# Six of the first MLP's last eight output tiles by seven products instead of eight, on one Trainium2 core

## The reference

```python
y_x = square(relu(modulate(x, g_pre_mlp, sh2, sc2) @ w_mlp_in)) @ w_mlp_out   # 1024 -> 4096 -> 1024
x = x + gt2 * rmsnorm(y_x, g_post_mlp)
...
proj = rmsnorm(x, norm_mix) @ w_in_2                                          # second block
k = rmsnorm((mem_h @ w_mem_kv)[:, keys], k_norm)                              # per head of 128
lb = cumsum(softmax(hg_lb_logits))                                            # lower bounds of the gates
```

## Time and profile before

| what | value |
|---|---|
| median of 3 runs | 1291.28 us (1291.2 to 1292.35) |
| the profiled execution | 1292.66 us, span 1291.4 us |
| busy share PE / PEld / DVE / ACT / POOL | 99% / 88% / 75% / 61% / 64% |
| granted TensorE clock | 1.00 throughout |
| last inner pair ends, first plain tile starts | 560.19 us |
| first half tile starts | 593.89 us |
| first half's statistic on PE | 601.45 us |
| rows of the next projection start | 606.25 us |

### The profile page before, as it was taken

One profiled execution on the slowest core, in us unless ns is written; L12 is line 12 of the kernel. 1 busy time (PEld: TensorE's weight loads), 2 busy tenths in 40 slices (PEclk: granted clock), 3 DMA queues, 4 the chain that ended last, 5 costly groups with the idle time before them and its releaser, 6 DMA issues.

```text
span 1291.4 us, 22880 instructions
## 1 busy us (share of the span) xinstructions
PE 1279.4 (99%) x8718; PEld 1136.7 (88%) x8718; DVE 965.1 (75%) x1685; ACT 781.8 (61%) x1488; POOL 824.5 (64%) x592
## 2 busy tenths in 40 slices
PE   9999999999999999999999999999999999999998
PEld 6788778879999999988788788777789999999998
DVE  5796795878778989834468575747589887987888
ACT  4532585479677585765655556645577655765664
POOL 2644334969778687656467373644378876877785
PEclk9999999999999999999999999999999999999999
DMA  9685235353333333432432122211223333333333
GB/s 378 238 311 215 88 124 210 114 180 108 122 105 101 101 99 112 173 105 98 131 100 82 47 66 66 66 66 33 66 82 114 100 99 102 108 103 115 99 105 108
DMA packets 42125, 156.35 MB, mean 121 GB/s; under 512 B 4384, under 2 KB 5152, under 8 KB 40992
## 3 DMA queue, kind: packets, MB, share of 16 engines
q1 hardware_dynamic: 41136, 151.60, 34.3%
q0 software_dynamic: 448, 2.62, 0.5%
q10 hardware_dynamic: 432, 0.67, 0.1%
HBM read 149.90 MB, written 4.19 MB: 119 GB/s over the span
## 4 chain that ended last, share of the span: by engine, by line
PE 78%; DVE 10%; POOL 5%; ACT 4%; issue 2%; DMA 1%; DVEq 0%; SPq 0%; ACTq 0%; POOLq 0%
PE bank L879 21%; PE bank L881 21%; PE bank L880 21%; PE bank L1437 2%; POOL wL L3803 2%; PE bank L928 1%; PE bank L930 1%; PE bank L929 1%; PE bank L982 1%; POOL acc L3813 1%; DVE small L2942 1%; POOL wL L3808 1%; PE bank L975 1%; PE bank L942 1%; PE bank L967 1%
## 5 line engine op out<-in xcount | busy, mean ns | idle before, releaser
L3803 POOL TENSOR_TENSOR wL<-raw,wH 128x1024 fp32r<-128x1024 f32 (+1 forms) x91 | 228.0, 2511 | 225.2 <-ACT wH L1815 222.1
L879 PE MATMUL bank<-hH,wH 128*128 128x512 f32 (+1 forms) x544 | 211.0, 388 | 1.7 <-POOL wL L3803 0.6
L881 PE MATMUL bank<-hH,wL 128*128 128x512 f32 (+1 forms) x544 | 200.6, 369 | 0.0
L880 PE MATMUL bank<-hL,wH 128*128 128x512 f32 (+1 forms) x544 | 200.4, 368 | 0.0
L3808 POOL TENSOR_TENSOR wL<-raw,wH 128x512 fp32r<-128x512 f32 (+1 forms) x120 | 154.6, 1289 | 31.1 <-ACT wH L1824 30.5
L879 PE MATMUL bank<-gH,wH 128*128 128x256 f32 x512 | 145.4, 284 | 0.3 <-POOL gL L3808 0.3
L880 PE MATMUL bank<-gL,wH 128*128 128x256 f32 x512 | 144.9, 283 | 0.0
L881 PE MATMUL bank<-gH,wL 128*128 128x256 f32 x512 | 144.9, 283 | 0.0
L1815 ACT ACTIVATE wH<-raw 128x1024 fp32r<-128x1024 f32 (+1 forms) x91 | 95.2, 1048 | 54.6 <-PE bank L881 28.3
L879 PEld LDWEIGHTS bank<-hH,wH 128*128 128x128 f32 x544 | 102.9, 189 | 25.1 <-issue 6.5
L881 PEld LDWEIGHTS bank<-hH,wL 128*128 128x128 f32 x544 | 102.6, 189 | 18.0
(11 more groups left out here) (537 smaller groups left out, 4086.1 us busy)
## 6 DMA issues: line engine op xcount, KB each, us to landing
raw<-in_wall SPq DMA_DIRECT2D x211, 512.0 KB, 3.3
rows<-in_wall SPq DMA_DIRECT2D x24, 1024.0 KB, 11.2
bra<-in_rpbw SPq DMA_DIRECT2D x8, 360.0 KB, 4.8
xq<-in_xt SPq DMA_DIRECT2D x2, 1024.0 KB, 6.8
xT<-in_xn SPq DMA_DIRECT2D x1, 2048.0 KB, 7.9
out_x<-xT SPq DMA_DIRECT2D x1, 2048.0 KB, 8.6
xT<-out_x SPq DMA_DIRECT2D x1, 2048.0 KB, 9.3
out_x<-xT SPq DMA_DIRECT2D x6, 256.0 KB, 2.4
```

The source lines that it names most:

```text
L879: matmul(o, a_h, b_h, start=first, stop=False)
L880: matmul(o, a_h, b_l, start=False, stop=False)
L881: return matmul(o, a_l, b_h, start=False, stop=last)
L3803: tt(wL[i % NHL][:, 0:n], raw[load(c) % NRAW][:, 0:n], wH[i % NHL][:, 0:n].bitcast(F32), ALU.subtract).then_inc(s.w_lo, 1)
```

## The change

The last quarter gets three outer pairs (12, 13, 14) for output tiles 0 to 5; tiles 6 and 7 stay plain and in halves. Forms 12 to 15 are now made as the others. What tiles 6 and 7 need beyond the forms, the late tokens of the even squares, is kept in `xlast` and split once (`late_high` on ACT, a rest on POOL). The keys are squared and split in two large operations (128x1024) instead of four small ones each; their statistics are two of 512 columns, after the sixth and the seventh product of pair 14, with roots of 512 columns on ACT and two scalings of 512 columns on DVE. Squares of the results go through two buffers `ysq` and are added up in `ysum` by POOL. The lower bounds are made during pairs 12 and 13. `xT` is read back in two halves after the last pair, ahead of the third chunk of the next projection.

```diff
-        if quarter < 3:
-            for j in range(4):
-                for i, odd in ((0, 0), (1, 0), (1, 1), (0, 1)):
-                    tile("w_mlp_out", 2 * j + i, range(8 * quarter + odd, 8 * quarter + 8, 2))
-        else:
-            group([("w_mlp_out", m) for m in range(2)], OUT_ORDER)
-            for m in range(2, 8):
-                tile("w_mlp_out", m, OUT_ORDER)
+        for j in range(4 if quarter < 3 else 3):
+            for i, odd in ((0, 0), (1, 0), (1, 1), (0, 1)):
+                tile("w_mlp_out", 2 * j + i, range(8 * quarter + odd, 8 * quarter + 8, 2))
+    for m in (6, 7):
+        tile("w_mlp_out", m, OUT_ORDER)
...
 # TensorE
+        KEY_PLACE = {(G - 1, 5): 0, (G - 1, 6): 1}
...
+                if (n, q) in KEY_PLACE:
+                    memory_statistic(KEY_PLACE[n, q])
...
-        outs = [claim(BANK["w_mlp_out", m]) for m in range(2)]
-        for i, k in enumerate(OUT_ORDER):
-            ...
-        for m in range(6):
-            b = BANK["w_mlp_out", m]
-            if m >= 2:
-                tile("w_mlp_out", m, OUT_ORDER, [(claim(b), XB)])
-            freed[b] = s.y_full, m + 1
-            if 0 < m < 5:
-                statistic_of_halves(f"mk{m - 1}", 256)
...
 # ScalarE, in the loop over the pairs
+            if not more:                               # the last pair, 14
+                first_product(n)
+                ahead("w_mlp_out", OUT_ORDER[0], 6, 2)
+                result_square(2)
+                result_square(3)
+                memory_root(0)
+                continue
...
             piece_high(n + 1, 2)
-            if c is not None and c < 12:
+            if c is not None:
                 sums_of_form_high(c, 0)
+            if outer_of(n) == 13:
+                late_high()
...
             piece_high(n + 1, 6)
+            if outer_of(n) == 13:
+                act.wait_ge(s.lb_v, 3)
+                activation(lb[:, 1, :], lb[:, 1, :], ACT.Exp).then_inc(s.lb_a, 1)
+                activation(lb[:, 2, :], lb[:, 2, :], ACT.Exp).then_inc(s.lb_a, 1)
+                result_square(0)
+                result_square(1)
+                memory_squares()
...
+        result_square(4)
+        result_square(5)
+        ahead("w_mlp_out", OUT_ORDER[0], 6)
+        memory_root(1)
+        act.wait_ge(s.piece_g, 5 * G)
+        for m in (6, 7):
+            act.wait_ge(s.y_full, m - 5)
+            square(tm[m - 4][:, 0:256], y[:, m, 0:256], s.sq)
...
+        def result_square(i):
+            act.wait_ge(s.y, Y.half + 24 + i + 1)
+            if i > 2:
+                act.wait_ge(s.add_g, ADD_G.f + i - 2)
+            square((ysq[i % 2] if i else ysum)[:, :], y[:, Y_ORDER[i], :], s.sq)
...
 # VectorE
+            if outer_of(n) == 12:
+                bounds_ahead()
+            if outer_of(n) == 13:
+                bounds()
...
+        added(G - 1, 2)
...
         last_tiles(0)
+        memory_key(0)
+        memory_key(1)
         dve.wait_ge(s.coef_c, 1)
-        dve.wait_ge(s.x_moved, 48)
         second_norm(0)
...
+                    dve.wait_ge(*((s.x_moved, 48) if n < 4 else (s.x_rest_in, 16)))
                     tt(b, xT[:, n, t], b, ALU.add).then_inc(s.add2, 1)
...
 # GpSimd
             if n + 1 == G:
-                ahead("w_mlp_out", 24, 0, 2)
+                pool.wait_ge(s.sums_hi, halved("mk1") + 1)
+                tt(ksqL[:, :], ksq[:, :], ksqH[:, :].bitcast(F32), ALU.subtract).then_inc(s.sums_lo, 2)
+                result_sum(1)
+                ahead("w_mlp_out", OUT_ORDER[0], 6, 2)
+                result_sum(2)
+                result_sum(3)
                 continue
...
             piece_rest(n + 1, 3)
+            if outer_of(n) == 13:
+                pool.wait_ge(s.full, FULL.b + 33)
+                rest(xlL[:, :, :], xlast[:, :, :], xlH[:, :, :], s.rest_g)
...
+        result_sum(4)
+        result_sum(5)
...
         late_squares(0)
+        ahead("w_mlp_out", OUT_ORDER[0], 6)
         ahead("w_in_2_first", 2, 14, 1)
         late_squares(1)
...
 # SyncE
-            if i == last_inner:
-                sp.wait_ge(s.prod, outer_done(2))
+            if i == first_f + 2:
+                sp.wait_ge(s.prod, 7 * G)
                 sp.wait_ge(s.x_moved, 32)
-                nc.sync.dma_start(xT[:, :, :], out).then_inc(s.x_moved, 16)
+                nc.sync.dma_start(xT[:, 0:4, :], out[:, 0:4, :]).then_inc(s.x_moved, 16)
+                nc.sync.dma_start(xT[:, 4:8, :], out[:, 4:8, :]).then_inc(s.x_rest_in, 16)
             weights_load(i)
```

More of the change, by code:

```diff
@@ L50 @@
 GROUPS = ((0, 8), (8, 16), (16, 22))
-OUT_ORDER = [24 + i for i in (0, 1, 2, 3, 4, 5, 7, 6)]
+OUT_ORDER = range(24, 32)
+Y_ORDER = (1, 0, 3, 2, 5, 4)
 def plan_weights():
@@ L146 @@
              for pair in [("inner", p) for p in range(max(0, 4 * quarter - 2), 4 * quarter + 2)]
-             + [("outer", 4 * quarter + j) for j in range(4 if quarter < 3 else 0)]]
+             + [("outer", 4 * quarter + j) for j in range(4 if quarter < 3 else 3)]]
 INNER = {i: at for at, (kind, i) in enumerate(FIRST_MLP) if kind == "inner"}
@@ L441 @@
 MULT = before(hc=8, h2=8, b=3)
-FULL = before(first=16, hm=8, h2=4, b=24, fs=22)
+FULL = before(first=16, hm=8, h2=4, b=33, fs=22)
 REST = before(first=8, hm=4, h2=8, fs=22)
-REST_G = before(first=8, hm=4, s2=4, b=24, form=4, fb=22)
+REST_G = before(first=8, hm=4, s2=4, b=33, form=4, fb=22)
 X2_S = before(x2=8, up=22)
@@ L469, in rooted @@
     return 2 * ROOTS.index(name) + 2
-HALVED = "mk0 mk1 mk2 mk3 lq".split()
+HALVED = "mk0 mk1 lq".split()
 def halved(name):
@@ L678, in build @@
     xl = at("xl", R + 92 * K, [128, 256])
+    xlast = at("xl", 88 * K, [128, 4, 256])
+    xlH = at("xlH", R + 56 * K, [128, 4, 256], F32R)
+    xlL = at("xlL", R + 60 * K, [128, 4, 256], F32R)
+    ysum = at("ysum", R + 72 * K, [128, 512])
+    ysq = [at("ysq", R + (74 + 2 * i) * K, [128, 512]) for i in range(2)]
     sS = [at("sS", R + (24 + 4 * i) * K, [128, 1024]) for i in range(2)]
@@ L1327, in tensor_program, with XB @@
             first_freed(n)
-        def XB(k):
-            return bH[:, k % 8, :], bL[:, k % 8, :], s.lo, LO.b + (k if k % 2 else k + 2)
-        outs = [claim(BANK["w_mlp_out", m]) for m in range(2)]
-        for i, k in enumerate(OUT_ORDER):
[L1334 to L1340, removed]
-        for m in range(6):
-            b = BANK["w_mlp_out", m]
-            if m >= 2:
-                tile("w_mlp_out", m, OUT_ORDER, [(claim(b), XB)])
-            freed[b] = s.y_full, m + 1
-            if 0 < m < 5:
-                statistic_of_halves(f"mk{m - 1}", 256)
+        def XB(k, i):
+            c = 12 + (k - 24) // 2
+            if k % 2:
+                return yH[:, c % 4, 256 + 256 * i:512 + 256 * i], yB[c % 4][:, i, :], s.lo, LO.b + 2 * c + 1
+            if i:
+                return xlH[:, c % 4, :], xlL[:, c % 4, :], s.rest_g, REST_G.b + 33
+            return yH[:, c % 4, 0:256], yA[c % 4][:, :], s.lo, LO.b + 2 * c + 2
         freed[2] = freed[3] = s.piece_v, 2 * G
@@ L2201, in first_result, with late_high, memory_squares, memory_root @@
             copy(y[:, m, :], sum_bank(n, (1, 3)[count - 1]), s.y)
[L2203 to L2206, removed]
+        def late_high():
+            act.wait_ge(s.relu_sq, 2 * 15)
+            act.wait_ge(s.prod, 7 * (INNER[13] + 1))
+            copy(xlH[:, :, :], xlast[:, :, :], s.full)
+        def memory_squares():
+            act.wait_ge(s.k_mem, 4)
+            activation(ksq[:, :], kvM[:, 0:2, :].rearrange("p a t -> p (a t)"), ACT.Square).then_inc(s.head_sq, 4)
+            act.wait_ge(s.head_sq, 4)
+            activation(ksqH[:, :], ksq[:, :], ACT.Copy).then_inc(s.sums_hi, 2)
+        def memory_root(i):
+            root_of(f"mk{i}", 128, kroot[:, 512 * i:512 * i + 512], bank[BANK["mk", i]])
+        def result_square(i):
[3 more added lines that the diff above has]
+            square((ysq[i % 2] if i else ysum)[:, :], y[:, Y_ORDER[i], :], s.sq)
         act.wait_ge(s.product, done("w_mlp_in", 7, 1))
@@ L2274, in scalar_program @@
                 nc.scalar.preload_act_table_set("natural_log_exp_and_others")
[L2276 to L2295, removed]
-                if m < 6:
-                    square(tm[t][:, :], y[:, m, :], s.sq)
-                    held[t] = s.add_g, ADD_G.f + m
-                else:
-                    square(tm[t][:, 0:256], y[:, m, 0:256], s.sq)
-            if 0 < m < 5:
-                if m > 1:
-                    act.wait_ge(s.mk_n, m - 1)
-                act.wait_ge(s.sums, 5 * G)
-                root(f"mk{m - 1}", 128, rs[(m - 1) % 2], 256)
-            if 0 < m < 4:
-                memory_square(m)
+        result_square(4)
[6 more added lines that the diff above has]
+            square(tm[m - 4][:, 0:256], y[:, m, 0:256], s.sq)
         root("post_a", 1024, bank[1], 256)
@@ L3246, in vector_program @@
             if c is not None:
-                if c < 12:
-                    form_sums(c)
+                form_sums(c)
                 odd_low(c)
```

(9 more changed lines are left out.)

154 lines of the change are left out of this document (69 added, 85 removed).

## The result

The changed kernel takes 1294.54 us (median of 12 runs, 1294.03 to 1295.53) against 1291.97 us for the kernel before (13 runs, 1291.2 to 1292.74). A thirteenth execution of the changed kernel, at 3634 us, is left out. The ratio is 1.0021 [1.0013, 1.0029]: slower by 0.2%, or 2.6 us. I predicted 1291.1 us and a range up to 1293.2. The time is outside it, on the side to which I had given 0.09.

The account below looks back on a forecast made before the run. PE, 99% busy, bounds the kernel. From the last inner pair's end to the first half's statistic (the marks), 20.16 + 0.39 + 20.55 = 41.10 us against 41.26, rounded to -0.2: 1291.1 us, range 1288.8 to 1293.2; z is pair 13's end.

Parts of the forecast that it names:

- the side to which I had given 0.09: Chance of a result slower by more than 0.2% (2.6 us), from x late and the unforeseen: 0.09.
- The step that failed: Pairs 12 to 14: bounds' operations and keys' roots and scalings run beside 10 us pairs, adding nothing to the path.
- The lock: Rival at the key scalings: two-SBUF-input DVE operations and POOL block each other, POOL late up to 0.8 us; chance 0.13.
- PE's list: PE in the last quarter: 33.70 us removed, 31.15 added, 2.55 less; 38.71 us between the marks if nothing waits.
- The 109 ns: Rival on the price per 256-column matmul, against 120 ns in the trace: would leave 3.57 us gained; chance 0.01.
- x came in time: Rival after the last pair: the read of `xT` lands late, norm 6.1 us late, 1297 us; chance 0.05.
- POOL's late queue: Last pair to the half's statistic: POOL's and ACT's queues make PE wait; it goes on 20.55 us after pair 13.
- Tile 6: Second wait, after pair 14: PE waits 0.56 us for POOL's low weights of tile 6; bounds 0 and 1.5.
- ACT's order: Ahead of the half's statistic: ACT's half squares stand behind a chunk's high part and a root, first ending at z + 19.7.
- POOL's sums alone: Lower bound at the half's statistic: with the half square already there, POOL's sums end at z + 19.85, no wait.
- The first wait: Start of the quarter's second outer pair, 13: POOL late, PE loses 0.39 us; bounds 0 and twice that.
- The third wait: Statistic of the first half: PE waits 1.45 us for POOL and ACT; bounds 0 and 2.9.

Follow-up runs that it names:

- experiment 3: Changed kernel with only pair 12's three bounds operations taken out (done far ahead, before the first block's norm), pair 13's kept: 1292.33 us.
- the second experiment: Changed kernel with two more 128x4 differences with two SBUF inputs added on DVE in pair 12, results unused: 1296.01 us.
- the seventh experiment: On top of experiment 1, ACT writes result squares to PSUM and DVE adds them; POOL keeps only tile 6's half square: 1289.98 us.
- experiment 1: Changed kernel with all the bounds' operations and their exponentials behind the second norm, the coefficient behind pair 14: 1292.13 us.
- experiment 6: On top of experiment 1, the high part of the next chunk on ACT goes behind the half squares of tiles 6 and 7: 1292.14 us.
- e4: Changed kernel with pair 13's bounds operations moved behind the second norm, pair 12's kept: 1294.35 us.
- e8: On top of experiment 1, three scratch differences of 128x4 with two SBUF inputs added on DVE in pair 12: 1294.40 us.

## Why the prediction was wrong

**The step that failed** is "The bounds' small operations and the keys' roots and scalings run beside 10 us pairs", priced at nothing because the last pair leaves DVE free. The reason is true of pair 14 and so of the operations of pair 13 (experiment 3). It is not true of those of pair 12, which stand ahead of DVE's weight sums for the last pair. The earlier trace rows had DVE busy 9.69 of 10.08 us in such a pair: 0.39 us of room, which three operations of 0.16 us overrun by 0.1 and two of 1.2 to 1.3 us by far. What the runs showed in place of "nothing" is 2.5 us of marks (44.04 with pair 12's operations, 41.54 and 41.52 without them).

**The lock was a rival at the wrong place.** I read its price from the earlier trace rows and gave it 0.13, but looked for it at the keys' scalings alone and took the excess for something that goes with the operation's size. It goes with the size of what POOL is running. At the scalings it was there as well, and cheap: beside them POOL's last sum took 1.69 us where the others take 1.29 to 1.30, and the half's sum 0.99 where the earlier trace rows have 0.74, together 0.64 us. In the changed kernel POOL's last sum and DVE's scalings are:

```profile
600.07 1.69 POOL L3925 TENSOR_TENSOR ysum<-ysum,ysq 128x512 f32<-128x512 f32 x1
```

```profile
599.88 0.75 DVE L3223 SCALAR_TENSOR_TENSOR kvM<-kvM,vecs,kroot 128x512 f32<-128x512 f32 x1
601.50 0.81 DVE L3223 SCALAR_TENSOR_TENSOR kvM<-kvM,vecs,kroot 128x512 f32<-128x512 f32 x1 [0.88 <-ACT kroot L1842]
```

So the two sides of the lock are both seen: whoever comes second waits, DVE in pair 12 and POOL at the scalings. In the second experiment POOL comes first at the scalings too, and there DVE waits. The Trainium skill (SBUF — State Buffer, Who interferes with whom) says this: the one that issues first has the shared ports for its whole instruction, and the other is fully blocked. The traces agree, down to operations of four elements in a partition. I had the rule and the row, and didn't go through the added DVE operations asking of each how many SBUF inputs it has and what POOL runs then. The same section of the Trainium skill says that `tensor_scalar` may also block through a mode of its own. The one with a single input in pair 13 took 1.22 us, up to the end of POOL's instruction, where the same one in the kernel before took 0.17 with POOL idle (565.09). That agrees; the reciprocal, at 0.18, wasn't held.

**What held.** PE's list: without waits the marks would be 38.71 apart, and the seventh experiment, with 0.69 us of waits, has 39.38. The distances between matmuls of 256 columns stay at 0.12 us. The 109 ns that the Trainium skill (TensorE: Matmul & The Clock Gate, Back-to-back issue gap) gives by its formula for the isolated gap are again not what the trace shows. x came in time: the read of `xT` is issued 12.3 us after z (592.13, for 10.7) and DVE's first read of it waits for no DMA. POOL's late queue: with the bounds out of the way (experiment 1) the statistic comes at z + 20.62 where I had z + 20.55. That POOL's and ACT's queues make PE wait there held; that the number came so close is luck. Tile 6 waits 0.22 us for 0.56, POOL's four sums take 6.02 us for 5.2 (0.39 of it the lock), and ACT's order, which I had as the last to end, isn't the limit (experiment 6). I had 0.70 us less if POOL's sums alone were the limit (z + 19.85), and the lock at the scalings added 0.64.

**What was mis-sized.** The first wait, taken over from the third quarter as 0.39, is 0.73 after and 0.68 to 0.76 in the experiments. Some 0.1 to 0.2 us of it lie 1.2 us ahead of pair 13's start, in the changed kernel at 568.40. POOL's two `ySL` parts of pair 12 end at 568.35, 9.40 us into the pair. Their like in the third quarter of the kernel before ended at 488.23, 9.07 us into its pair, which began at 479.16:

```profile
485.68 2.55 POOL L3808 TENSOR_TENSOR ySL<-yS,yH 128x512 fp32r<-128x512 f32 x2 [1.80 <-ACT yH L1824]
```

So 0.33 us of POOL's lateness answers to the 0.34 us of wait. That the one makes the other isn't shown, and what makes POOL later there wasn't tried. With the first experiment's 0.76 for this term my sum is 41.10 + 0.37 = 41.47, and that experiment has 41.54.

The account in us of marks: the edit of PE's list -2.55; first wait +0.7; POOL's queue ahead of the statistic some +2.1, which together leave the +0.3 of experiment 1; the lock in pair 12 +2.5; sum +2.8. The third wait was mis-sized too, 1.45 for 1.85, and in the changed kernel the weights of tile 6 made PE wait 1.19 us for 0.56, because the lateness from pair 12 came on top.

## What to carry to other kernels

Where GpSimd works without a break, price each DVE operation with two SBUF inputs (and, by one row here, a `TENSOR_SCALAR` from SBUF to SBUF) at up to one whole GpSimd instruction, however few elements it has; put such operations where GpSimd is idle, or where nothing waits for DVE. Before taking matmuls out of a list that is 99% busy, add up what the other engines must do before the next point at which PE needs them: here 2.55 us of matmuls gave nothing until the sums had left GpSimd's queue. A wait in the middle of a chain is repaired on the engine that comes last, and moving work ahead on the other one shows which that is.

## What the runs showed of the hardware

A DVE operation of 128x4 with two SBUF inputs took 0.15 to 0.16 us with POOL idle, and 1.00 to 1.55 us, up to the end of POOL's instruction, with POOL at work; one of 128x8 took 2.42 us under an instruction of 128x1024 and 0.16 with POOL idle. Where three or four stood one behind the other and POOL's instructions were back to back, the first began 0.1 to 0.2 us before POOL's instruction ended and took 0.15 to 0.19 us (after, e2, e4, e8); each of those behind it waited for one whole instruction of POOL, as long as POOL had one to run.

In the second experiment the granted clock fell. Its windows before and behind 592 us (busy PE, PEld, DVE, ACT, POOL, clock, DMA share, GB/s):

```profile
585.00:592.00 7.00, 4.60 (x34) 4.16 (x34) 6.86 (x8) 5.22 (x8) 7.00 (x5) 1.00 0.23 78
592.00:596.00 4.00, 4.00 (x20) 3.49 (x19) 3.86 (x8) 1.84 (x3) 4.00 (x3) 0.57 0.21 37
```

For some 3.3 us the matmuls of 256 columns started 0.21 us apart instead of 0.12; a mean of 0.57 is mostly the lower level, 1.2 GHz. Just before, PE had been busy for only 4.60 of 7.00 us. The slower matmuls cost the marks nothing: PE still waited 1.05 us for POOL at the statistic, and they only took their part out of that wait. The changed kernel, with shorter waits at the same places, kept 1.00 throughout.
